# Two gathers and two selections one expert group later, the first later part one group earlier

## The chip, the cores and the metric

The kernel runs on one core of one Trainium2 chip. The metric is the device time of one execution in microseconds, the median of several. The engines are TensorE (PE; its weight loads are PEld), VectorE (DVE), ScalarE (ACT), GpSimd (POOL) and SyncE (SP), which only issues DMAs here. Every engine works through its own list in order, and they meet at semaphores.

## The reference

Two transformer blocks on 256 tokens of width 1024, in float32. The part that matters here is the mixture of experts of the first block. Each token picks one of 4 groups of 8 experts, then the two best experts in it:

```
grp  = argmax(softmax(h @ w_group + b_group))
top_p, top_e = top_k(softmax(in_grp), 2)
weights = p_grp * top_p / sum(top_p)
for each expert e, for its tokens x:
    a = silu(x @ w_gate[e]) * (x @ w_up[e])
    y[token] += weight * (a @ w_down[e])
```

There are 32 experts, w_gate and w_up 1024 x 256 and w_down 256 x 1024 each, so 100 MB of weights for this part. The other stages (projections, mLSTM, attention, the second block with its feed-forward) are not touched.

## The kernel before

The experts are worked through in blocks of 32 tokens. Four blocks side by side fill the 128 columns of a matmul's output, so a group of four experts is one unit. The first 32 tokens of every expert are the groups 0 to 7. An expert with more tokens has further blocks; up to 15 of them stand in the groups 8 to 11, the later groups. `ORDER` (L57) is the order of the twelve: 0, 1, 2, 8, 3, 9, 4, 5, 10, 6, 11, 7; o is the place in it, and two neighbours in it are a pair q.

A normal group is `gate_up(o, k)` for k = 0 to 3 (L1338), each 16 matmuls on one piece of weights, then `hidden_columns` (two transposes of the activation), then `down_rows` (L1414), 32 matmuls on two more pieces. Between these stands `scatter(o - 1)` (L1367), which adds the outputs of the group before to the tokens' rows in PSUM. A later group is cut into three parts: `later_part(g, 0)` and `(g, 1)` are gate and up, `(g, 2)` is `hidden_columns`, a scatter and the down product. `AFTER` (behind the first gate_up of a normal group), `INSIDE` (behind its last) and `BEHIND` (behind its down product) say where they stand (L59 to 61).

The inputs of a pair are gathered by matmuls with a selection matrix: `gather(q, i, b)` (L1296), i = 0 to 3, eight matmuls each, copied out by ACT and DVE in `gathered`. `early_gather` (L1456) waits first until DVE has read the last down product from the two banks that are used again. `GATHERS` (L62) says in which group a pair is gathered. `selects(o)` (L1461) turns the selection matrices of a pair and computes its weights, in the place that `SELECTS` (L63) gives; POOL's `select_pair(q + 2)` (L2284) waits for that and makes the matrices of a later pair.

Weights come in two streams. SP loads 48 pieces of 2 MB, six to a group, in order (L676 to 707). From piece 9 on four slots in `big` take turns (piece 13 alone goes to `dring`), and a piece is issued only when TensorE has used the piece before it in its slot:

```
if n >= SLOTS:
    sp.wait_ge(s_used, slot_before(n) + 1)
```

The weights of a later part are fetched by POOL with indirect DMAs of 128 rows of 8 KB, one for each block, four for a part (three in group 11), in `later_piece(g, k)` (L2303). Where a block is not needed, its index lies out of bounds and its rows bring nothing. The part (8, 0) waits for the seventh piece used, (8, 1) for the fourteenth (numbers 0 to 13: that is the second gate_up of group 2), each further one for the part two before it. POOL's list mixes these issues with `select_pair` (L2318 to 2334). TensorE waits for all blocks of a part in `landed_later` (L1332).

In front of the last two gate_ups of group 7 stand 7 and 13 matmuls on zeros (`filler`), whose only effect is that TensorE is busy.

Of the kernel before, what the change touches and what calls it, by code (L numbers as in the profile page):

```python
# [55 lines left out]
ONCE = SLOTS + RING  # L56
ORDER = [0, 1, 2, 8, 3, 9, 4, 5, 10, 6, 11, 7]  # L57
NLATER = 3
INSIDE = {2: (8, 0), 3: (9, 0), 4: (9, 2), 5: (10, 1), 6: (11, 0), 7: (11, 2)}  # L59
AFTER = {3: (8, 2), 4: (9, 1), 5: (10, 0), 6: (10, 2), 7: (11, 1)}  # L60
BEHIND = {2: (8, 1)}
GATHERS = {1: 1, 2: 2, 3: 3, 4: 4, 6: 5}  # L62
SELECTS = {0: 0, 1: 1, 2: 2, 4: 3, 6: 4, 9: 5}  # L63
LATE = (3, 6, 8, 11)
BESIDE = [(0, 1), (2, 3), (4,), (5,), (6, 7), (8, 9), (10,), (11,)]
NPAIR = NALL // 2
# [86 lines left out]
def build(nc, x, consts, vecs, rows, mod, wa, experts, pieces, wb, ffn, out):  # L153
    with ExitStack() as ctx:
# [162 lines left out]
        def gate_up_done(eng, g):  # L317

            if g < NGRP:
                eng.wait_ge(s_used, NPIECE * g + 4)  # L320
            else:
                eng.wait_ge(s_lused, NLATER * (g - NGRP) + 2)
# [444 lines left out]
        def _(pe):  # L767
# [521 lines left out]
            gathered, downs = {}, []  # L1289
# [166 lines left out]
            def early_gather(q, i):  # L1456

                pe.wait_ge(s_ot, len(downs))
                gather(q, i, 6 + i % 2)
# [10 lines left out]
            for g in range(NGRP):  # L1470
                o = ORDER.index(g)
                q = GATHERS.get(g)
                for k in range(4):
                    if g == NGRP - 1 and k >= 2:
                        pe.wait_ge(s_ot, len(downs))
                        filler(6 * k - 5, 6)
                    gate_up(o, k)
                    if g == 0 and k < 2:
                        gather(0, 2 + k, 6 + k)
                    if k == 0 and g in AFTER:  # L1480
                        later_part(*AFTER[g])
                    if q and k in (1, 2):
                        early_gather(q, k - 1)
                if q and g != 4:
                    early_gather(q, 2)
                    early_gather(q, 3)
                if g in INSIDE:
                    later_part(*INSIDE[g])
                if g == 0:
                    selects(o)  # L1490
                    hidden_columns(o)
                elif g == 4:
                    hidden_columns(o)
                    early_gather(q, 2)
                    early_gather(q, 3)
                    scatter(o - 1)
                    selects(o)
                elif g == NGRP - 1:
                    hidden_columns(o)
                else:  # L1500
                    scatter(o - 1)
                    hidden_columns(o)
                    selects(o)
                down_rows(o)
                if g == NGRP - 1:
                    scatter(o - 1)
                if g in BEHIND:
                    later_part(*BEHIND[g])
# [16 lines left out]
            for i in range(2):  # L1525
                pe.wait_ge(s_cw[i], 16 * (i + 1))
                for j in range(CB // 2):
                    w = ckw[:, j] if i == 0 else cvw[j // 8][:, j % 8]
                    q, at = j % 4, (CB // 2 * i + j) * KVG * NC
# [29 lines left out]
            for t in range(NT):  # L1559
                for h in range(NSAH):  # L1560
                    g, r = h // 3, h % 3
                    q = fmT[g * HD:(g + 1) * HD, 10 + r, t * P:(t + 1) * P]
# [154 lines left out]
        def _(act):  # L1717
# [295 lines left out]
            def gathered(q, i, b):  # L2013

                act.wait_ge(s_ga2, 4 * q + i + 1)
                xg_free(act, q)
                for c in (2 * i, 2 * i + 1):
                    ins = nc.scalar.activation(xg[q % 2][:, c, :], ps[:, b, (c % 2) * T:(c % 2 + 1) * T], ACT.Identity,
                                               scale=modT[:, 40 + c:41 + c], bias=modT[:, 16 + c:17 + c])
                ins.then_inc(s_xa, 1)  # L2020
# [29 lines left out]
            for o, g in enumerate(ORDER):  # L2050
                b = 4 if g < NGRP else 5
                q = GATHERS.get(g)
                if o >= 1 and o not in LATE:
                    outputs_high(o - 1)
                if g == 9:
                    gathered(4, 0, 6)
                if q and g != 4:
                    gathered(q, 0, 6)
                gate_up_done(act, g)
                if o >= 1:  # L2060
                    act.wait_ge(s_hid2, o)
                nc.scalar.activation(hid[:, 0, :], ps[:, b, 0:T], ACT.Tanh, scale=0.5).then_inc(s_hth2, 1)
                if o in LATE and g >= NGRP:
                    outputs_high(o - 1)
                if q and g != 4:
                    gathered(q, 2, 6)
                if o == 0:
                    rows_turned(o)
                act.wait_ge(s_at, o + 1)
                nc.scalar.copy(aT[:, :, :], ps[:, b, 0:T].rearrange("p (f n) -> p f n", f=2)).then_inc(s_atc, 1)  # L2070
                if o in LATE and g < NGRP:
                    outputs_high(o - 1)
                if g == 4:
                    gathered(q, 2, 6)
                if o:
                    rows_turned(o)
            last_high()
# [166 lines left out]
        def _(pool):  # L2244
# [39 lines left out]
            def select_pair(q):  # L2284

                if q >= 1:
                    pool.wait_ge(s_stw, 2 * q)
                for k in range(2):
                    for t in range(NT):
                        for h in range(2):  # L2290
                            g = ORDER[2 * q + h]
                            ins = nc.gpsimd.tensor_scalar(sel12[:, k, t, h * P:(h + 1) * P], const("iota"),  # L2292
                                                          gsp[:, k, t, g:g + 1], None, ALU.is_equal)
                            if (k, t, h) == (1, NT - 1, 1):
                                link(ins)
                            else:
                                link.later(ins)
                if q >= 2:
                    pool.wait_ge(s_ga2, 4 * (q - 1))
                nc.gpsimd.tensor_tensor(sel[:, q % 2, :, :], sel12[:, 0, :, :], sel12[:, 1, :, :], ALU.add  # L2300
                                        ).then_inc(s_sel, 1)

            def later_piece(g, k):  # L2303

                n = later_number(g, k)
                if n == 0:
                    pool.wait_ge(s_used, FIRST.index(6) + 1)
                elif n == 1:
                    pool.wait_ge(s_used, max(SLOTS, ONCE + 1))
                else:  # L2310
                    pool.wait_ge(s_lused, n - 1)
                for b in range(later_blocks(g)):
                    pool.indirect_dma_start(
                        later_slot(n, b), None, later_rows,
                        bass.IndirectOffsetOnAxis(ap=xidx[:, QUAD * (g - NGRP) + b, k:k + 1], axis=0),
                        bounds_check=NE * P * NLATER - 1, oob_is_err=False).then_inc(s_later[n % 2], 16)
# [10 lines left out]
            select_pair(4)  # L2327
            later_piece(9, 2)
            later_piece(10, 0)
            select_pair(5)  # L2330
            later_piece(10, 1)
            later_piece(10, 2)
            for k in range(3):
                later_piece(11, k)
            power(small[:, 24:28], small[:, 24:28], 4, s_ms, 4, s_rstd)
# [10 lines left out]
        def _(dve):  # L2346
# [484 lines left out]
            def gathered(q, i, b):  # L2831

                dve.wait_ge(s_ga2, 4 * q + i + 1)
                xg_free(dve, q)
                for c in (2 * i, 2 * i + 1):
                    ins = V.tensor_scalar(xg[q % 2][:, c, :], ps[:, b, (c % 2) * T:(c % 2 + 1) * T],
                                          modT[:, 40 + c:41 + c], modT[:, 16 + c:17 + c], ALU.mult, ALU.add)
                ins.then_inc(s_xv, 1)
# [48 lines left out]
            for o, g in enumerate(ORDER):  # L2887
                b = 4 if g < NGRP else 5
                q = GATHERS.get(g)
                if o >= 1 and o not in LATE:  # L2890
                    outputs_low(o - 1)
                if g == 9:
                    gathered(4, 1, 7)
                if q and g != 4:
                    gathered(q, 1, 7)
                dve.wait_ge(s_hth2, o + 1)
                if o >= 1:
                    dve.wait_ge(s_at, o)
                link(V.scalar_tensor_tensor(hid[:, 1, :], hid[:, 0, :], 1.0, ps[:, b, 0:T], ALU.add, ALU.mult))
                V.tensor_tensor(hid[:, 1, :], hid[:, 1, :], ps[:, b, T:2 * T], ALU.mult).then_inc(s_hid2, 1)  # L2900
                if o in LATE:
                    outputs_low(o - 1)
                if q:
                    gathered(q, 3, 7)
                if o in SELECTS:
                    p = SELECTS[o]
                    slot_weights(2 * p, 6)
                    slot_weights(2 * p + 1, 7)
# [494 lines left out]
```

## Time and profile before

| | |
|---|---|
| median of 3 runs | 1025.64 us |
| lowest, highest | 1022.02, 1027.52 us |
| the profiled execution | 1023.9 us, span 1022.1 us |
| TensorE busy | 972.6 us, 95% of the span |
| DVE, ACT, POOL busy | 48%, 38%, 37% |
| mean granted clock | 0.98 |
| moved by DMA | 252.08 MB, mean 247 GB/s; by POOL's queue (q0, software) 3.17 MB |

The expert stage lies from about 347 to 570 us of the span. A busy TensorE is no proof that it is the bound: its share is a mean over stages. The page's slices give the engines' busy tenths, the DMA engines' share and the GB/s for 40 equal slices; the timeline of an engine shows in brackets how long it was idle before an instruction and what ended that.

### The profile page before, as it was taken

To read this page: it belongs to the slowest core of one execution; us is meant where nothing else is said; L and a number is where in the kernel's file an instruction comes from. 1 tells how busy PE (TensorE), PEld (TensorE's weight loads), DVE (VectorE), ACT (ScalarE), POOL (GpSimd) and SP (SyncE) were. 2 spreads that over 40 slices of the span, in tenths; PEclk is the share of its full clock that TensorE was granted. 3 is DMA by queue.
4 is the path that set the end of the run, shared out by engine and by line. 5 is a ranking of instruction groups with operands and counts; after the bars stand their busy time and mean duration, and the time that the engine had idled before them with its cause. 6 is when DMAs were issued, how large, how long until landed. Compare 5 with 4: busy or idle time off the path is not lost.

```text
span 1022.1 us, 15203 instructions
## 1 busy us (share of the span) xinstructions
PE 972.6 (95%) x6120; PEld 713.1 (70%) x6120; DVE 492.0 (48%) x853; ACT 385.7 (38%) x617; POOL 379.7 (37%) x249
## 2 busy tenths in 40 slices
PE   7999999999999999898699999999999999999997
PEld 3887777777788544344243699777556789999996
DVE  1445358544244622213031603536665368777775
ACT  1633345445433321111020644544553254434342
POOL 0885747444783055453320499740002500000000
PEclk7999999999999999999799999999999999999999
DMA  9996955334469999999999888533224465454521
GB/s 377 345 414 266 372 172 158 87 100 124 144 208 427 360 425 423 416 398 370 407 407 414 310 321 255 156 93 103 86 80 144 165 268 195 176 204 165 205 82 41
DMA packets 49274, 252.08 MB, mean 247 GB/s; under 512 B 10432, under 2 KB 11072, under 8 KB 31424
## 3 DMA queue, kind: packets, MB, share of 16 engines
q1 hardware_dynamic: 42736, 248.10, 64.4%
q0 software_dynamic: 6480, 3.17, 1.1%
q8 instruction: 41, 0.67, 0.3%
q14 instruction: 17, 0.14, 0.0%
HBM read 294.22 MB, written 1.05 MB: 289 GB/s over the span
## 4 chain that ended last, share of the span: by engine, by line
PE 76%; DVE 7%; issue 6%; DMA 4%; ACT 3%; POOL 2%; DVEq 0%; SPq 0%; POOLq 0%; ACTq 0%
PE ps L885 33%; PE ps L1208 17%; PE ps L1347 3%; PE ps L781 2%; PE ps L1423 2%; PE ps L1362 2%; PE ps L1374 2%; PE ps L833 1%; PE ps L1304 1%; DMA tail<-in_experts_dram,xidx 1%; PE ps L1438 1%; DMA big<-in_pieces_dram 1%; DMA xs<-in_x_dram 1%; PE ps L895 1%; POOL sel L2292 1%
## 5 line engine op out<-in xcount | busy, mean ns | idle before, releaser
L2262 POOL TENSOR_TENSOR wl<-ring,wh 128x1024 fp32r<-128x1024 f32 (+5 forms) x132 | 289.3, 2211 | 228.9 <-ACT wh L1760 227.1
L1760 ACT ACTIVATE wh<-ring 128x1024 fp32r<-128x1024 f32 (+5 forms) x148 | 143.4, 983 | 132.1 <-PE ps L885 100.9
L885 PE MATMUL ps<-wh,hTh 128*128 128x512 f32 (+3 forms) x384 | 153.0, 398 | 1.3 <-DVE wl L3086 1.3
L885 PE MATMUL ps<-wl,hTh 128*128 128x512 f32 (+3 forms) x384 | 148.3, 386 | 0.0
L885 PE MATMUL ps<-wh,hTl 128*128 128x512 f32 (+3 forms) x352 | 136.7, 388 | 0.0
L1208 PE MATMUL ps<-hTs,wsp 128*128 128x256 f32 x1056 | 128.7, 284 | 0.5 <-DVE wsp L2922 0.5
L1208 PEld LDWEIGHTS ps<-hTs,wsp 128*128 128x128 f32 x1056 | 128.1, 192 | 1.5 <-DVE wsp L2922 0.7
L2250 POOL TENSOR_TENSOR small<-small 128x2 f32<-128x2 f32 (+2 forms) x7 | 5.3, 759 | 272.7 <-DVE small L3235 192.4
L885 PEld LDWEIGHTS ps<-wh,hTh 128*128 128x128 f32 x384 | 73.0, 190 | 22.7 <-issue 6.8
L885 PEld LDWEIGHTS ps<-wl,hTh 128*128 128x128 f32 x384 | 73.0, 190 | 13.5
L885 PEld LDWEIGHTS ps<-wh,hTl 128*128 128x128 f32 x352 | 66.8, 190 | 13.4
L1208 PE MATMUL ps<-wsp,aTs 128*128 128x512 f32 x264 | 61.7, 391 | 0.0
L1347 PE MATMUL ps<-big,xg 128*32 128x512 f32 x432 | 53.7, 605 | 7.3 <-DMA big<-in_pieces_dram 7.0
L885 PE MATMUL ps<-hTh,wh 128*128 128x256 f32 x208 | 58.1, 279 | 0.0
L885 PE MATMUL ps<-hTl,wh 128*128 128x256 f32 x208 | 58.0, 279 | 0.0
L885 PE MATMUL ps<-hTh,wl 128*128 128x256 f32 x208 | 57.6, 277 | 0.0
L1976 ACT ACTIVATE wsp<-ring 128x2048 fp32r<-128x2048 f32 x22 | 42.0, 1909 | 40.4 <-PE ps L1208 34.1
L1208 PEld LDWEIGHTS ps<-wsp,aTs 128*128 128x128 f32 x264 | 49.0, 188 | 9.7
L2922 DVE TENSOR_TENSOR wsp<-ring,wsp 128x2048 fp32r<-128x2048 f32 x22 | 50.3, 2285 | 9.5 <-ACT wsp L1976 9.5
L2292 POOL TENSOR_SCALAR sel<-cst,few 128x128 fp32r<-128x128 f32 x40 | 23.3, 596 | 58.6 <-PE ps L1316 58.6
L885 PEld LDWEIGHTS ps<-hTh,wh 128*128 128x128 f32 x208 | 39.1, 188 | 0.8 <-issue 0.8
L885 PEld LDWEIGHTS ps<-hTl,wh 128*128 128x128 f32 x208 | 39.1, 188 | 0.0
(481 smaller groups left out, 1637.3 us busy)
## 6 DMA issues: line engine op xcount, KB each, us to landing
big<-in_pieces_dram SPq DMA_DIRECT2D x42, 2048.0 KB
ring<-in_wa_dram SPq DMA_DIRECT2D x68, 512.0 KB, 3.9
big<-in_mod_dram SPq DMA_DIRECT2D x11, 2048.0 KB, 10.4
ring<-in_ffn_dram SPq DMA_DIRECT2D x11, 2048.0 KB, 9.1
ring<-in_wb_dram SPq DMA_DIRECT2D x40, 512.0 KB, 3.9
dring<-in_ffn_dram SPq DMA_DIRECT2D x11, 1024.0 KB, 4.9
ring<-in_wb_dram SPq DMA_DIRECT2D x12, 384.0 KB, 5.7
dring<-in_pieces_dram SPq DMA_DIRECT2D x2, 2048.0 KB, 21.4
```

The costliest lines, as they stand in the source:

```text
L781: mm = pe.matmul(ps[32 * q:32 * q + 32, 6, :], condw[:, c, :], mtile[n][:, c, :], start=(c < 4), stop=(c >= 4), skip_group_check=True)
L885: mm = pe.matmul(out, x[i], y[j], start=(p, c, k) == (0, 0, 0), stop=(c, k) == (KD - 1, 2), skip_group_check=True)
L1208: mm = pe.matmul(out, w[a], x[b], start=start and n == 0, stop=stop and n == 2, skip_group_check=skip)
L1347: mm = pe.matmul(ps[b * BS:(b + 1) * BS, 4, :], xg[q % 2][:, c, at:at + BS], slot_part(s, b)[:, cc * 512:(cc + 1) * 512], start=(c == 0), ...
L1362: mm = pe.matmul(ps[b * BS:(b + 1) * BS, 5, :], xg[q % 2][:, c, at:at + BS], later_slot(later_number(g, k), b)[:, cc * 512:(cc + 1) * 512] ...
L1374: mm = pe.matmul(ps[:, 2 * t + n, :], selT[:, (o // 2) % 2, o % 2, t * P:(t + 1) * P], x[:, n * 512:(n + 1) * 512], start=False, stop=Fals ...
L1423: mm = pe.matmul(ps[b * BS:(b + 1) * BS, 6 + n, :], aT[:, f, b * BS:(b + 1) * BS], slot_part(s, b)[:, n * 512:(n + 1) * 512], start=(f == ...
L1760: nc.scalar.activation(quarter(name, q, "high"), quarter(name, q, "raw"), ACT.Copy).then_inc(s_qh, 1)
L1976: nc.scalar.activation(wsp[:, 0 if last else m, 0, :], src, ACT.Copy).then_inc(s_hi[m], 1)
L2262: nc.gpsimd.tensor_tensor(quarter(name, q, "low"), quarter(name, q, "raw"), quarter(name, q, "high"), ALU.subtract).then_inc(s_ql, 1)
L2292: ins = nc.gpsimd.tensor_scalar(sel12[:, k, t, h * P:(h + 1) * P], const("iota"), gsp[:, k, t, g:g + 1], None, ALU.is_equal)
L2922: V.tensor_tensor(wsp[:, dst, 1, :], src, wsp[:, dst, 0, :], ALU.subtract).then_inc(s_lo[m], 1)
```

## The change

Two later-part tables change: (8, 0) moves from in front of group 2's down product (INSIDE[2]) to the end of group 1 (BEHIND[1]). The gathers 2 and 3 of the pair 4 move from group 4, behind its hidden columns, to group 5, behind its second and third gate_up; their copies on ACT and DVE move with them. In SELECTS the entry 6: 4 becomes 7: 4, so the two selections of pair 4 (`select_rows` 8 and 9) go from group 4 (o = 6) to group 5 (o = 7). In POOL's list `select_pair(5)` goes behind the issues of (10, 1) and (10, 2).

```diff
-INSIDE = {2: (8, 0), 3: (9, 0), 4: (9, 2), 5: (10, 1), 6: (11, 0), 7: (11, 2)}
+INSIDE = {3: (9, 0), 4: (9, 2), 5: (10, 1), 6: (11, 0), 7: (11, 2)}
 AFTER = {3: (8, 2), 4: (9, 1), 5: (10, 0), 6: (10, 2), 7: (11, 1)}
-BEHIND = {2: (8, 1)}
+BEHIND = {1: (8, 0), 2: (8, 1)}
 GATHERS = {1: 1, 2: 2, 3: 3, 4: 4, 6: 5}
-SELECTS = {0: 0, 1: 1, 2: 2, 4: 3, 6: 4, 9: 5}
+SELECTS = {0: 0, 1: 1, 2: 2, 4: 3, 7: 4, 9: 5}
...
                     if q and k in (1, 2):
                         early_gather(q, k - 1)
+                    if g == 5 and k in (1, 2):
+                        early_gather(4, k + 1)
...
                 elif g == 4:
                     hidden_columns(o)
-                    early_gather(q, 2)
-                    early_gather(q, 3)
                     scatter(o - 1)
                     selects(o)
...
+                if g == 5:
+                    gathered(4, 2, 6)
                 gate_up_done(act, g)
...
-                if g == 4:
-                    gathered(q, 2, 6)
...
             later_piece(10, 0)
-            select_pair(5)
             later_piece(10, 1)
             later_piece(10, 2)
+            select_pair(5)
...
+                if g == 5:
+                    gathered(4, 3, 7)
                 dve.wait_ge(s_hth2, o + 1)
...
-                if q:
+                if q and g != 4:
                     gathered(q, 3, 7)
```

## Rows read from the trace of the kernel before

**Rows 1.** From the page: DMA engines' share in 40 slices, and the pieces' issues.
```profile
DMA  9996955334469999999999888533224465454521
...
big<-in_pieces_dram SPq DMA_DIRECT2D x42, 2048.0 KB
```

**Rows 2.** Windows: length, busy PE, PEld, DVE, ACT, POOL, clock, DMA share, GB/s.
```profile
420.00:430.00 10.00, 9.13 (x68) 3.64 (x72) 2.51 (x2) 1.96 (x3) 2.37 (x3) 0.83 1.02 416
...
445.00:448.00 3.00, 3.00 (x32) 1.10 (x28) 0.84 (x1) 0.00 (x0) 2.92 (x6) 1.00 0.75 246
477.00:480.00 3.00, 3.00 (x34) 1.13 (x30) 0.00 (x0) 0.00 (x0) 3.00 (x6) 1.00 0.43 85
510.00:512.00 2.00, 2.00 (x24) 0.65 (x20) 0.39 (x1) 0.00 (x0) 0.00 (x0) 1.00 0.73 128
```

**Rows 3.** Timeline of SP: start us, length us, queue, line, what it issues.
```profile
427.98 0.37 SPq L701 DMA_DIRECT2D big<-in_pieces_dram  x1
445.43 0.37 SPq L701 DMA_DIRECT2D big<-in_pieces_dram  x1
478.51 0.37 SPq L701 DMA_DIRECT2D big<-in_pieces_dram  x1
510.22 0.37 SPq L701 DMA_DIRECT2D big<-in_pieces_dram  x1
```

**Rows 4.** Timeline of POOL: the first issue of later parts (8,0), (8,1), (8,2), (9,2), (10,1).
```profile
369.81 1.26 POOL L2313 DMA_INDIRECT ring<-in_experts_dram,xidx  x1 [2.87 <-issue]
388.42 1.09 POOL L2313 DMA_INDIRECT dring<-in_experts_dram,xidx  x1 [2.16 <-PE ps L1347]
401.14 0.99 POOL L2313 DMA_INDIRECT ring<-in_experts_dram,xidx  x1 [7.75 <-PE ps L1362]
449.35 1.09 POOL L2313 DMA_INDIRECT dring<-in_experts_dram,xidx  x1 [0.16 <-issue]
482.43 1.09 POOL L2313 DMA_INDIRECT dring<-in_experts_dram,xidx  x1 [0.16 <-issue]
```

**Rows 5.** Timeline of PE in groups 2 and 3.
```profile
383.95 1.93 PE L1347 MATMUL ps<-big,xg 128*32 128x512 f32 x16
392.74 1.92 PE L1347 MATMUL ps<-big,xg 128*32 128x512 f32 x16 [1.01 <-DMA big<-in_pieces_dram]
404.21 3.64 PE L1423 MATMUL ps<-big,aT 128*32 128x512 f32 x32 [0.41 <-ACT selT L2025]
407.64 0.63 PE L1362 MATMUL ps<-dring,xg 128*32 128x512 f32 x2
420.87 5.34 PE L1438 MATMUL ps<-ring,aT 128*32 128x512 f32 x32 [3.45 <-issue]
```

**Rows 6.** The chain that ended last: start us, length us, what it ran through.
```profile
486.41 13.14 DMA tail<-in_experts_dram,xidx
521.79 1.14 PE ps L1304 x8
```

**Rows 7.** Timeline of PE in groups 4, 5 and 7.
```profile
465.90 0.62 PE L1438 MATMUL ps<-dring,aT 128*32 128x512 f32 x2 [0.85 <-issue]
474.76 0.38 PE L1314 MATMUL ps<-cst,selt 128*128 128x128 f32 x2
476.53 3.64 PE L1423 MATMUL ps<-big,aT 128*32 128x512 f32 x32 [0.41 <-ACT selT L2025]
492.38 2.80 PE L1347 MATMUL ps<-big,xg 128*32 128x512 f32 x16 [3.62 <-DMA big<-in_pieces_dram]
499.59 1.07 PE L1362 MATMUL ps<-dring,xg 128*32 128x512 f32 x2 [4.41 <-DMA tail<-in_experts_dram,xidx]
554.12 1.92 PE L1347 MATMUL ps<-big,xg 128*32 128x512 f32 x16
```

**Rows 8.** Timeline of DVE behind the down product of (9, 2).
```profile
469.60 1.28 DVE L2860 SCALAR_TENSOR_TENSOR olt<-ps,few,gateb 128x1024 f32<-128x1024 f32 x1 [4.82 <-PE ps L1438]
472.00 1.23 DVE L2865 TENSOR_TENSOR ol__69<-olt,oh__67 128x1024 fp32r<-128x1024 f32 x1 [1.12 <-ACT oh__67 L2032]
```

## The prediction

> **What bounds the kernel now.** I read the page's slices first, then the ten-microsecond windows, then the queues of SP and POOL, then TensorE in order of time, then the chain. TensorE is busy nearly everywhere, but [rows 1] show the DMA engines full (9 or 8 in every slice from about 310 to 590 us): in the expert stage weights come at some 420 GB/s [rows 2]. A piece is 2048 KB [rows 1], so at 420 GB/s it takes 5.0 us, and 48 pieces take 240 us. The stage ends when the piece stream ends, and the stream is late only by the time in which no piece has been asked for. From 350 us to the last pieces the full windows break three times: 445 to 448 is 0.75 full, 477 to 480 is 0.43, 510 to 512 is 0.73 [rows 2]; that is 0.75, 1.7 and 0.5 us by the share, and with the slow ends of each (a piece asked for at 478.51 finds an engine share that recovers at about 479.8, 1.3 us later) I count 1.3, 2.9 and 1.3 us, 5.5 in all. I number the pieces 0 to 47, six to a group. A piece is asked for when TensorE has finished with the piece before it in its slot; [rows 3] are the issues of pieces 23, 26, 32 and 38. So TensorE sets when pieces are asked for, and the pieces set when it may go on: near the end piece 45 is used at 554.12 [rows 7], right behind 13 fillers, and what comes behind it is TensorE's own.
>
> The later parts are the second resource. POOL issues four blocks for each, and TensorE may use them only when all have landed. The part (8, 1) is first issued at 388.42 [rows 4] and used at 407.64 [rows 5], 19.2 us later, with TensorE's weight load at its wait; (8, 2) is issued at 401.14 and used at 420.87, 19.7 us later and 13.2 us behind the part before, after a stop of 3.45 us; (9, 2) is issued at 449.35 and used at 465.90 [rows 7] after a short stop, 16.5 us; (10, 1) is issued at 482.43 and used at 499.59 after a stop of 4.41 us, 17.1 us. The chain of waits goes through that last one, with 13.14 us from its fourth issue on [rows 6]; POOL could not issue it earlier, as it first made the sixth pair's selection matrices, for which it waits for TensorE's selections.
>
> **The change part by part.** All times are of the profiled execution: span 1022.1, own time 1023.9, which is 1.7 us under the median of 1025.64.
>
> (1) The first later part, (8, 0), comes straight behind the fifth and sixth pieces of group 1, at 383.95, where now group 2 begins [rows 5]. Nothing of its transfer moves: first issue at 369.81 [rows 4]. By the row of (8, 1) it lands at 369.8 + 19.2 = 389.0; by the shortest case, 16.5, at 386.3. So a wait of 2.4 to 5.1 us is added; I take 5.1, since (8, 1) is its neighbour under the same load. Behind it on TensorE stand all of group 2 and every release of a slot. In the trace a stop of 3.45 us is followed by 32 matmuls in 5.34 us against 3.64 for the same count at full clock [rows 5], with a granted clock of 0.83 in 420 to 430 [rows 2], that is, some time at 1.2 GHz; so the part costs 5.3, and TensorE begins group 2 at 394.4, 10.4 us later than now.
>
> (2) What group 2 then loses. Now from 383.95 to its down product at 404.21 are 20.3 us, of which 1.0 is a wait for a piece and 3.6 the part that has left: 15.7 remain, so the down product starts at 410.1, 5.9 late. It ends at 413.5. But (8, 1) is issued only when the second piece of group 2 is used, which is 4.5 us after group 2's start (388.42 less 383.95): at 398.9 instead of 388.4. It lands 19.2 later, at 418.1: a wait of 4.6. With 5.3 for it (slow again) and 1.9 for the next piece, TensorE reaches the scatter in front of (8, 2) at 425.3 and is done with that at 427.6. (8, 2) is issued at some 404 by the order of POOL's queue. It lands at 404 + 19.7 = 423.7 if parts overlap, or 13.2 behind the part before, at 431.3, if they go one after the other. I take 431.3: the longest time from issue belongs to the one part that was issued while its forerunner was under way. Then 5.3 of work: done at 436.6, against 426.2 now: 10.4 late. With the early landing and full clock it is 431.4, 5 late.
>
> (3) What the stream loses. Counting back from 445.5, where it runs dry, by 5.0 a piece and 2.5 for the MB of a real block (POOL's queue moved 3.17 MB in all, the table above has it, so one block of the later groups is real and brings one MB in each of (8, 0), (8, 1) and (8, 2)), piece 17 must follow piece 16 at 395.5 when (8, 1) comes later. It is asked for at 396.4 instead of 385.9 (its slot's piece is the first of group 2, used from 383.95 for 1.93 [rows 5]) and starts 1.3 behind: 2.2 us dry. Piece 22 then ends at 432.7. Piece 23 is asked for when the second piece of group 3 is used, 10.4 later than 427.98, so at 438.4: 7.0 dry. Piece 26, now at 445.43, comes at 455.8, with the stream at 454.7: 2.4 dry. Together 11.6 against 1.3: the stream is 10.3 late at piece 26; by the early ends of (1) and (2) about 2.5 only.
>
> (4) What the other moves give back. In group 4 two gathers (1.14 us each, eight matmuls, [rows 6]) and two selections (with the copy behind them 1.8 us, from 474.76 to 476.53, [rows 7]) leave the stretch in front of the down product that starts at 476.53. What they covered comes out: behind (9, 2)'s down product the output, its high part and its low part (3.7 us from the matmuls' end on DVE and ACT, [rows 8]) must be there for the scatter. (9, 2), issued 10.4 later, lands at 476.3, its product ends at 479.9; 3.7 for the parts and 0.9 for the second half of the scatter give 484.6, so 8.1 late instead of 10.3: the move is worth 2.2. Piece 32 is asked for at 486.6 and the stream is dry for only 0.6 to 0.9 instead of 2.9. In group 5 the two gathers lie where TensorE now waits 3.62 us for piece 33 [rows 7]: free. POOL's sixth pair of selection matrices no longer stands in front of (10, 1), so its transfer is asked for when (9, 2) is done, near 481, and lands near 498; TensorE comes to it at 502 behind piece 33. The stop of 4.41 and its slow matmuls (5.6 for 3.6) go. What is late next is piece 33. The selections then cost their 1.8 in front of the down product of group 5: it starts at 509 to 510 against 507.90, and piece 38 is asked for before the stream, now later, has run dry: 1.3 saved. After that pieces come at 5.0 us each; from the third part of group 6 on TensorE waits for them, as it nearly does now.
>
> **Sum.** Now piece 38 starts 1.3 behind its issue at 510.22, at 511.5, and piece 45 ends eight pieces later, at 551.5. After the change piece 32 starts at 486.6 + 1.3 = 487.9 and 14 pieces follow without a break: piece 45 ends at 557.9, 6.4 later. (By the dry time alone: 2.2 + 7.0 + 2.4 + 0.8 = 12.4 against 5.5, 6.9.) TensorE takes piece 45 2.6 us behind its end now, and waits for piece 33 until 2.6 behind its end (479.8 + 10.0 against 492.38), for the piece at 392.74 until 2.2 behind: 0 to 0.4 of slack, which I take off. +6.0 us. Own time 1029.9; on the median 1031.6.
>
> One place of the Trainium skill speaks for another outcome. The notes, DMA: Bandwidth & Descriptors, section Anatomy of one DMA, give about 2.0 us and bytes / 436e3 for a transfer issued from GpSimd; an estimate by it for four blocks of 1 MB is 11.6 us, and (8, 0) would be there at 381.4, before TensorE asks. This case's trace does not agree: 16.5 to 19.7 us from first issue to use, with a full piece stream beside it. The result of that rule is the first rival, priced below from rows.
>
> **Rivals.** A, faster: (8, 0) has landed at 383.95 (a transfer of 14.1 us or less from its first issue). Then no stop is added, group 2 only exchanges order, (8, 2) is issued earlier, and the late dry spells (2.9 and 1.3) go: 4.2 less, 1021.4. It decides at 383.95. Against it: no row has less than 16.5. For it: no row shows when (8, 0) lands, as it is used long after; and a late start of TensorE may cost less, since 3.45 of waiting in group 3 goes. Chance 0.1. B, even: parts overlap and the stops are short, (8, 2) lands near 424. Then the stream is dry 2.5 to 4 more by piece 26 and gets back 4: -1 to +2.5, 1026.5 in the middle. Chance 0.27. C, the reverse of step (4): the new order does not take the stop at (10, 1) away, because piece 33 and POOL's queue leave it late, and the early loss stands in full: +9 to +10, 1035. Chance 0.13. The forecast itself 0.5.
>
> **Numbers.** A measurement of this kernel tells 0.5% (5.1 us) from no change. The forecast (its own range +3 to +8, 1028.6 to 1033.6) gives 0.32 slower and 0.18 within; B gives 0.26 within and 0.01 faster; C 0.13 slower; A 0.05 faster and 0.05 within. Together faster 0.06, within 0.49, slower 0.45. The range leaves out half of A and the end of C: 1022.5 to 1036.
>
> **What would show it.** Right: TensorE stops some 5 us in front of the first L1362 matmuls, now at about 384, and they take over 5 us; it stops again in front of the next two later parts; SP asks for piece 23 near 438 and the DMA share dips near 433 to 439; the stop at (10, 1) is gone, the dip at 477 is nearly gone; the last filler ends near 560. Wrong: (8, 0) running at 384 without a stop, or a DMA share that stays full from 390 to 445.

## The result, and the profile after

The changed kernel is slower: 1027.56 us in the median of 19 runs against 1022.02 for the kernel before, ratio 1.005 with an interval of 1.0034 to 1.0066, that is 5.1 us (3.5 to 6.7). (One of the 19 executions took 5402.69 us and does not count in the ratio.) The ratio is estimated from the executions of both kernels and need not be the quotient of the two medians; where this text gives a difference in us, it is worked out from the ratio. The profiled execution after has a span of 1023.9 us, only 1.8 more than before. A single pair of executions is a poor measure here: in the one before, TensorE's clock fell to 1.2 GHz twice in the second block, where it did not in the one after. The expert stage itself is 3.8 us longer, counted from the start of group 1's down product to the first matmul on piece 45: 173.60 us before (380.52 to 554.12) and 177.41 after (379.86 to 557.27). The stage began 0.66 us earlier in the execution after, and what follows piece 45 took 1.35 us less there; that is how 3.8 becomes 1.8.

TensorE in order of time, after; the columns are those of [rows 5].

```profile
388.51 6.18 PE L1362 MATMUL ps<-ring,xg 128*32 128x512 f32 x32 [5.01 <-DMA ring<-in_experts_dram,xidx]
394.52 1.89 PE L1347 MATMUL ps<-big,xg 128*32 128x512 f32 x16
...
409.90 3.64 PE L1423 MATMUL ps<-big,aT 128*32 128x512 f32 x32 [0.41 <-ACT selT L2025]
...
416.57 0.62 PE L1362 MATMUL ps<-dring,xg 128*32 128x512 f32 x2 [3.03 <-DMA tail<-in_experts_dram,xidx]
...
429.81 3.64 PE L1438 MATMUL ps<-ring,aT 128*32 128x512 f32 x32 [1.75 <-issue]
...
473.34 0.62 PE L1438 MATMUL ps<-dring,aT 128*32 128x512 f32 x2 [2.58 <-issue]
...
479.55 1.17 PE L1374 MATMUL ps<-oh__67,selT 128*128 128x512 f32 x4 [2.21 <-ACT oh__67 L2032]
...
481.85 3.64 PE L1423 MATMUL ps<-big,aT 128*32 128x512 f32 x32
...
496.74 1.92 PE L1347 MATMUL ps<-big,xg 128*32 128x512 f32 x16 [0.25 <-DMA big<-in_pieces_dram]
498.48 0.60 PE L1362 MATMUL ps<-dring,xg 128*32 128x512 f32 x2
...
505.98 3.86 PE L1423 MATMUL ps<-big,aT 128*32 128x512 f32 x32 [0.41 <-ACT selT L2025]
...
512.77 3.33 PE L1347 MATMUL ps<-big,xg 128*32 128x512 f32 x16 [2.94 <-DMA big<-in_pieces_dram]
...
557.27 1.92 PE L1347 MATMUL ps<-big,xg 128*32 128x512 f32 x16
```

TensorE stops 5.01 us in front of (8, 0) and the part's 32 matmuls then take 6.18 us. Group 2 starts at 394.52 instead of 383.95. (8, 1) and (8, 2) are waited for as well (3.03, 1.75), (9, 2) for 2.58. Where the row says "<-issue", the view names no cause; that the wait in front of (8, 2) is for its transfer can be read from the landing: its last block landed at 429.61, and the matmuls start at 429.81. In the same way (8, 0) landed at 388.47 and (8, 1) at 416.52. The scatter of group 4 waits 2.21 us for the output that the two gathers and the selections had covered. The stop of 4.41 at (10, 1) [rows 7] is gone, and of the wait of 3.62 for piece 33 only 0.25 is left. In their place TensorE now waits 2.94 us at 512.77 for piece 36, the first of group 6, and the 16 matmuls behind that wait take 3.33 us instead of 1.9. Group 6 had no such wait before.

The clock at the first stop, then the DMA engines in the windows where they now have too little to do; columns as in [rows 2].

```profile
386.00:394.00 8.00, 5.49 (x28) 1.33 (x32) 1.19 (x1) 0.00 (x0) 0.00 (x0) 0.57 1.01 425
...
394.00:400.00 6.00, 6.00 (x56) 2.26 (x52) 0.00 (x0) 0.69 (x2) 1.03 (x1) 1.00 0.68 233
432.00:438.00 6.00, 6.00 (x56) 2.32 (x48) 2.51 (x2) 2.08 (x3) 3.13 (x3) 1.00 0.54 155
450.00:456.00 6.00, 5.59 (x55) 2.27 (x58) 1.92 (x5) 0.72 (x3) 5.52 (x9) 1.00 0.72 240
484.00:487.00 3.00, 3.00 (x32) 0.91 (x28) 1.28 (x1) 0.13 (x1) 0.00 (x0) 1.00 0.99 252
...
380.00:556.00 176.00, 152.57 (x1167) 65.71 (x1164) 40.61 (x70) 26.69 (x50) 64.96 (x77) 0.96 0.98 397
```

The same before, with the whole of each dip of [rows 2]:

```profile
442.00:450.00 8.00, 7.59 (x75) 3.46 (x77) 2.36 (x6) 2.06 (x4) 6.60 (x10) 1.00 0.90 353
476.00:482.00 6.00, 5.59 (x54) 2.12 (x57) 1.85 (x5) 0.82 (x2) 5.69 (x9) 1.00 0.64 206
509.00:514.00 5.00, 4.62 (x42) 1.24 (x34) 1.32 (x2) 1.07 (x2) 0.57 (x1) 1.00 0.86 274
...
380.00:556.00 176.00, 154.69 (x1191) 67.78 (x1190) 40.97 (x72) 27.04 (x51) 65.09 (x77) 0.96 0.99 406
```

Two dips are new (near 396 and 434), the one at 452 is the old one of 445, that of 477 [rows 2] has shrunk to a short one at 485, and that of 510 has gone. The granted clock of 0.57 around the stop says that most of that stretch was at 1.2 GHz; TensorE had been idle for 5 us in it. By the bytes that are missing against 420 GB/s the four dips are 2.7, 3.8, 2.6 and 1.2 us, 10.2 together, against 1.3, 3.1 and 1.7 before, 6.1: 4.1 us of dry stream more. Over the whole of 380 to 556 us the mean fell from 406 to 397 GB/s, which is 3.8 us of a full stream, as much as the stage is longer.

The issues of SP and POOL that follow from it (after): piece 23, asked for at 427.98 before [rows 3], piece 26 (445.43) with the two behind it, piece 32 (478.51); then the first issues of (8, 0), (8, 1), (8, 2) and (10, 1) [rows 4].

```profile
435.22 3.38 SPq L701 DMA_DIRECT2D big<-in_pieces_dram  x2
...
452.67 3.80 SPq L701 DMA_DIRECT2D big<-in_pieces_dram  x3
...
483.83 0.37 SPq L701 DMA_DIRECT2D big<-in_pieces_dram  x1
```

```profile
369.16 1.26 POOL L2313 DMA_INDIRECT ring<-in_experts_dram,xidx  x1 [2.87 <-issue]
...
398.97 1.09 POOL L2313 DMA_INDIRECT dring<-in_experts_dram,xidx  x1 [13.38 <-PE ps L1347]
...
404.25 0.99 POOL L2313 DMA_INDIRECT ring<-in_experts_dram,xidx  x1 [0.30 <-issue]
...
477.79 0.98 POOL L2313 DMA_INDIRECT dring<-in_experts_dram,xidx  x1 [11.05 <-PE ps L1438]
```

POOL waited 13.38 us for the second piece of group 2 before it could ask for (8, 1); before, 2.16 us [rows 4]. Piece 23 was asked for 7.2 us later, and that is the dip at 434. And (10, 1) was asked for at 477.79 instead of 482.43, with nothing of POOL's matrices in front of it.

The two stretches of the second block in which the clock fell before (same columns):

```profile
680.00:686.00 6.00, 6.00 (x26) 4.29 (x25) 3.14 (x8) 2.47 (x10) 0.14 (x1) 0.72 0.00 0
...
769.00:774.00 5.00, 4.44 (x12) 3.45 (x13) 4.69 (x9) 0.00 (x0) 0.00 (x0) 0.66 0.64 269
```

In the execution after, the clock is 1.00 in both windows. That part of the kernel is the same program in both, so the profiled execution of before was a little unlucky there.

### The profile page after: what moved, and what is told of

Read it like the earlier page. It is cut to its first block, busy times and chain, and to the rows that moved or that the text cites. A ratio compares the mean times of both kernels' runs of the same rounds, so it can differ in the third digit from the quotient of the medians.

```text
span 1023.9 us, 15195 instructions
## 1 busy us (share of the span) xinstructions
PE 968.2 (95%) x6112; PEld 709.4 (69%) x6120; DVE 493.8 (48%) x853; ACT 385.6 (38%) x617; POOL 380.2 (37%) x249
## 4 chain that ended last, share of the span: by engine, by line
PE 74%; DMA 10%; DVE 8%; issue 4%; ACT 3%; POOL 1%; DVEq 0%; SPq 0%; POOLq 0%; ACTq 0%
PE ps L885 31%; PE ps L1208 17%; DMA big<-in_pieces_dram 4%; PE ps L1347 4%; PE ps L1362 2%; PE ps L781 2%; DMA ring<-in_wa_dram 2%; PE ps L1374 2%; PE ps L1423 2%; DMA ring<-in_experts_dram,xidx 1%; PE ps L833 1%; PE ps L1438 1%; DMA tail<-in_experts_dram,xidx 1%; PE ps L1304 1%; DMA xs<-in_x_dram 1%
## 5 line engine op out<-in xcount | busy, mean ns | idle before, releaser
L885 PEld LDWEIGHTS ps<-hTh,wl 128*128 128x128 f32 x208 | 39.6, 191 | 0.0
```

Of the source, the lines that this page charges most:

```text
L885: mm = pe.matmul(out, x[i], y[j], start=(p, c, k) == (0, 0, 0), stop=(c, k) == (KD - 1, 2), skip_group_check=True)
```

## The experiments

The theory: (8, 0) in front of group 2 makes TensorE wait for a transfer, and what stands behind it (the releases of group 2's slots, hence (8, 1), (8, 2), the pieces) comes late; the late moves bring something. The main rival: the late moves are what costs. The runs stand in three series, each on a chip of its own with the kernel before beside it: rest_only, part_only, mid_part and one_block in the first, fill_stop, select_only, gather_only and mid_only in the second, rest_again, mid_again and select_mid in the third. All ratios are to the kernel before of the same series, with their 95% intervals. "Stage" is the time from the start of group 1's down product to the first matmul on piece 45 in the one profiled execution, 173.60 us before. One execution can lie several us beside the median: use the stage to see where time goes, and the ratio for how much.

**Late moves alone (rest_only, rest_again).** Against the changed kernel:

```diff
-INSIDE = {3: (9, 0), ...
-BEHIND = {1: (8, 0), 2: (8, 1)}
+INSIDE = {2: (8, 0), 3: (9, 0), ...
+BEHIND = {2: (8, 1)}
```

> The change without its first part: (8, 0) stays in front of group 2's down product; the two gathers, the two selections and POOL's order are moved. Theory (the loss is the stop in front of (8, 0)): faster than the kernel before by 2 to 4 us (0.2 to 0.4%), no stop at (10, 1), the dip of the DMA share at 477 to 480 shorter by 2 us. Rival 1 (the late moves cost: the scatter of group 4 has lost its cover): slower than before by 1 to 5 us. Rival 2 (the late moves do nothing, as the stream covers them): within 1 us of before.

Measured: 1020.21 against 1023.53, ratio 0.9974 (0.9963 to 0.9984), 2.7 us faster; stage 168.22 us. TensorE, in the place where the stops at piece 33 and (10, 1) were, has one short wait, and after it the down product of group 5 starts at 496.35 instead of 507.90:

```profile
487.11 1.92 PE L1347 MATMUL ps<-big,xg 128*32 128x512 f32 x16 [1.17 <-DMA big<-in_pieces_dram]
...
496.35 3.64 PE L1423 MATMUL ps<-big,aT 128*32 128x512 f32 x32 [0.41 <-ACT selT L2025]
```

Rival 1 falls: the late moves do not cost. The profiled execution was the fastest of its 13 (1015.47 us), so a stage of 168.22 is too good. The second run, in the third series:

> The late moves alone, a second time, beside the next two on one chip: -2 to -4 us against before.

Measured: 1018.52 against 1023.62, 0.9946 (0.9927 to 0.9966), 5.5 us faster, more than expected; the two intervals only just meet (0.9963 to 0.9966). So the worth of the late moves is some 3 to 5 us, and two series can differ by about as much as an interval is wide; stage 171.75 this time, in the slowest of the 10 executions. The expected shorter dip at 477 to 480 is seen in the first of the two traces (none is left there) and not in the second:

```profile
476.00:482.00 6.00, 6.00 (x51) 1.92 (x53) 1.28 (x1) 0.10 (x1) 0.66 (x1) 0.95 0.60 168
```

What both have is that the stop at (10, 1) and the dip at 510 are gone; both wait for piece 36 instead (2.21 and 2.95 us).

**(8, 0) alone (part_only).** The kernel before with only

```diff
-INSIDE = {2: (8, 0), 3: (9, 0), ...
-BEHIND = {2: (8, 1)}
+INSIDE = {3: (9, 0), ...
+BEHIND = {1: (8, 0), 2: (8, 1)}
```

> The kernel before with only the move of (8, 0) to the end of group 1. Theory: slower than the kernel before by 6 to 9 us (0.6 to 0.9%), more than the whole change, with a stop of 5 us at 384, dips of the DMA share near 396, 434 and 453, and the stop at (10, 1) kept or turned into one behind pieces. Rival 1 (the late moves are what costs): within 1 us of before. Rival 2 (late moves do nothing): the same as the whole change, +5 us.

Measured: 1030.14 against 1023.53, 1.0062 (1.0045 to 1.0079), 6.3 us slower, more than the whole change; stage 180.50. The stop and the slow matmuls, and two of the dips:

```profile
389.28 6.43 PE L1362 MATMUL ps<-ring,xg 128*32 128x512 f32 x32 [4.83 <-DMA ring<-in_experts_dram,xidx]
```

```profile
396.00:399.00 3.00, 3.00 (x32) 0.69 (x24) 0.00 (x0) 0.00 (x0) 0.00 (x0) 1.00 0.26 63
484.00:487.00 3.00, 3.00 (x32) 1.09 (x28) 0.00 (x0) 0.00 (x0) 3.00 (x6) 1.00 0.41 82
```

The dip at 484 is that of 477 [rows 2] moved on by 7 us: without the late moves nothing of it is given back. The stop at (10, 1) is kept, as expected, and is 5.30 us long. The two halves do not quite add up: +6.3 with -2.7 or -5.5 gives +3.6 or +0.8, less than the +5.1 of the whole; with the intervals the first fits and the second hardly.

**(8, 0) two gate_ups later (mid_part, mid_again).** The changed kernel with

```diff
-BEHIND = {1: (8, 0), 2: (8, 1)}
+BEHIND = {2: (8, 1)}
...
+                    if (g, k) == (2, 1):
+                        later_part(8, 0)
```

> The whole change, but (8, 0) stands behind the second gate_up of group 2, so that the piece that (8, 1) waits for is used first. Theory: TensorE comes to (8, 0) at 387.5, waits about 1.5 us, full clock after it, (8, 1) is issued at 388.4 as before: the loss is gone, 1 to 4 us faster than the kernel before. Rival 1: as slow as the whole change, +5 us. Rival 2: as the kernel before.

Measured: 1019.52 against 1023.53, 0.995 (0.993 to 0.9971), 5.1 us faster, a little more than expected; stage 170.72.

```profile
389.25 3.64 PE L1362 MATMUL ps<-ring,xg 128*32 128x512 f32 x32 [1.60 <-DMA ring<-in_experts_dram,xidx]
```

A stop of 1.60 and full clock after it. The wait for the transfer ends near 389, as in the changed kernel; 3.6 us of work put in front of the wait, and with it the piece that (8, 1) waits for, turn +5 into -5. The second run:

> The late moves with (8, 0) behind the second gate_up of group 2, a second time. If the place of (8, 0) is worth something by itself beside the late moves, 1 to 3 us faster than the late moves alone; if the 2.4 us between the two in the first call were noise, the same as they.

Measured: 1018.3 against 1023.62, 0.9935 (0.9911 to 0.996), 6.6 us faster; the late moves alone gave 0.9946 in the same series. The intervals overlap widely: the place of (8, 0) has no worth that this shows.

**One block instead of four (one_block).** The changed kernel, with three empty transfers of (8, 0) left out:

```diff
                 blocks = sum(later_blocks(NGRP + m // NLATER) for m in range(n % 2, n + 1, 2))
+                if n % 2 == 0:
+                    blocks -= QUAD - 1
...
-                for b in range(later_blocks(g)):
+                for b in range(1 if n == 0 else later_blocks(g)):
```

> The whole change, but POOL issues only the first of the four blocks of (8, 0) and TensorE waits for that one; the other three bring nothing in either kernel. Theory: the block lands near 380.5, no stop at 384, group 2 begins at 387.4 with full clock, (8, 1) is issued at 392 instead of 399; the result is at or below the kernel before, -3 to 0 us. Rival 1: +5 us as the whole change, without the stop. Rival of mechanism (the stop is harmless, what costs is that group 2's releases come 3.6 us later because of the part's own matmuls): +3 to +5 us.

Measured: 1022.08 against 1023.53, 0.9993 (0.9978 to 1.0007), 0.7 us faster; stage 174.73.

```profile
384.38 3.64 PE L1364 MATMUL ps<-ring,xg 128*32 128x512 f32 x32
387.81 1.93 PE L1349 MATMUL ps<-big,xg 128*32 128x512 f32 x16
...
424.77 6.13 PE L1440 MATMUL ps<-ring,aT 128*32 128x512 f32 x32 [3.83 <-issue]
```

```profile
392.29 1.09 POOL L2315 DMA_INDIRECT dring<-in_experts_dram,xidx  x1 [5.60 <-PE ps L1349]
```

```profile
431.00:434.00 3.00, 3.00 (x28) 1.44 (x24) 1.87 (x2) 1.26 (x2) 1.98 (x2) 1.00 0.44 74
```

The stop is gone, and some 5.8 us of the loss with it (+5.1 has become -0.7, the two in different series), so the wait was for this transfer, and for its empty blocks: the last packet of the one real block ended at 380.70. But the kernel still has only 0.7 of the 3 to 5 us that the late moves bring. (8, 1) is asked for at 392.29 instead of 388.42, as (8, 0)'s own 3.6 us lie in front of group 2, (8, 2) still stops TensorE for 3.83, and the stream is dry at 431 to 434. So the rival of mechanism holds a part: the order costs some 2 to 4 us even without the stop. (In the same series rest_only is 1.9 us faster than this kernel, with intervals that just overlap, and mid_part 4.4 us, with intervals apart.)

**Busy during the stop (fill_stop).** The changed kernel with

```diff
+                if g == 1:
+                    pe.wait_ge(s_ot, len(downs))
+                    filler(16, 6)
                 if g in BEHIND:
                     later_part(*BEHIND[g])
```

> The whole change, with a wait for DVE's read of the down product and 16 matmuls on zeros in front of (8, 0), so that TensorE is busy during most of the stop. Theory, with the clock as a part of the loss: the stop itself stays (group 2 cannot begin before (8, 0) has landed near 388.5), but the 32 matmuls of (8, 0) take 3.6 us instead of 6.2 and the granted clock stays at 2.4 GHz there: 1 to 2.5 us faster than the whole change, so +2.5 to +4 against the kernel before. Rival (only the wait matters, the clock does not reach the end): +5 us as the whole change.

Measured: 1026.06 against 1023.13, 1.0028 (1.0013 to 1.0043), 2.9 us slower; stage 174.79.

```profile
384.27 3.40 PE L895 MATMUL ps<-zero 128*128 128x512 bf16 x15 [1.63 <-DVE olt L2863]
387.95 3.64 PE L1362 MATMUL ps<-ring,xg 128*32 128x512 f32 x32 [0.28 <-DMA ring<-in_experts_dram,xidx]
```

```profile
384.00:392.00 8.00, 7.45 (x55) 2.81 (x60) 1.23 (x1) 1.06 (x1) 0.74 (x1) 1.00 1.01 424
```

The clock stays at 1.00, the part takes 3.64 instead of 6.18. That 2.5 us are saved at the place is shown. The end says about 2.2 us (1.005 against 1.0028), as was expected, but the two ratios come from different series and their intervals overlap: that some 2 us of the loss are the clock that falls behind the stop is likely, not shown.

**The late moves one by one (select_only, gather_only).** The kernel before with only `SELECTS` and POOL's `select_pair(5)` moved:

> The kernel before with only the selections of pair 4 and POOL's sixth pair of matrices one group later; the gathers stay in group 4, (8, 0) stays in group 2. Theory: the stop at (10, 1) goes, and 1.8 us leave the stretch in front of group 4's down product, of which most is taken by the wait for the output; piece 32 is asked for 1 to 1.5 us earlier: 1.5 to 2.5 us faster than before. Rival: all of the gain of the late moves is in the gathers, 0 to -0.5 us here.

Measured: 1020.21 against 1023.13, 0.9967 (0.9947 to 0.9986), 3.4 us faster, more than expected; stage 170.88. (10, 1) is asked for at 470.44, and TensorE uses it at 490.99 without a wait:

```profile
470.44 0.99 POOL L2313 DMA_INDIRECT dring<-in_experts_dram,xidx  x1 [12.50 <-PE ps L1438]
```

```profile
490.99 0.60 PE L1362 MATMUL ps<-dring,xg 128*32 128x512 f32 x2
```

The gain does not come by the whole of the expected way. Group 4's down product starts 95.9 us into the stage against 96.0 before, and piece 32 is asked for at 97.9 against 98.0: in these two executions the selections that have left group 4 bring nothing there. What is won is won behind, at (10, 1). With only the gathers moved:

> The kernel before with only the two gathers moved to group 5. Theory: the gathers leave group 4 (2 us and 1 us of wait), but the stop at (10, 1) stays, with POOL's selection matrices earlier by the same 1 to 2 us: 0.5 to 2 us faster than before. Rival: the stop at (10, 1) eats it, within 0.5 us.

Measured: 1022.41 against 1023.13, 0.9994 (0.9976 to 1.0012), no difference; stage 173.53. The wait for piece 33 is gone, and the stop at (10, 1) has grown from 4.41 to 6.02 us, as the expectation's rival had it:

```profile
498.31 1.07 PE L1362 MATMUL ps<-dring,xg 128*32 128x512 f32 x2 [6.02 <-DMA tail<-in_experts_dram,xidx]
```

So the gain of the late moves is that of the selections and POOL's order, moved together; which of the two it is was not tried apart. The gathers alone only move TensorE ahead to a wait that they cannot shorten.

**The middle place alone (mid_only), and with the selections (select_mid).** The edits are those above, on the kernel before.

> The kernel before with only (8, 0) moved behind the second gate_up of group 2. Theory: if the place is harmless and frees the ring slots for (8, 2) no earlier in effect, 0 to -1 us against before, since the gain of 5 us seen with all moves together comes from the late ones (2.7 measured) and from an earlier (8, 2) (up to 2). Rival: the place itself brings 2 us or more by itself.

Measured: 1024.13 against 1023.13, 1.0007 (0.9992 to 1.0023), no difference, as expected. The trace shows why an earlier (8, 2) is worth nothing. It is asked for 7 us earlier than before (401.14) and used no earlier than before (420.87):

```profile
394.19 0.99 POOL L2315 DMA_INDIRECT ring<-in_experts_dram,xidx  x1 [0.30 <-issue]
```

```profile
421.33 5.34 PE L1438 MATMUL ps<-ring,aT 128*32 128x512 f32 x32 [3.14 <-issue]
```

> Only the selections late, and (8, 0) behind the second gate_up of group 2; the gathers stay in group 4. If the gain is all in the selections and POOL's order, the same as the other two, -3 to -4 us against before; if the gathers add a part, 1 us behind the run above.

Measured: 1017.74 against 1023.62, 0.9948 (0.9924 to 0.9972), 5.3 us faster, like the other two of its series, and more than expected. The three are one result: some 0.5% faster than the kernel before and 1% faster than the changed one, and the only part they share is the selections with POOL's order. The simplest version that beats both kernels is therefore select_only.

## Why the prediction was right

The forecast was +6.0 us by a stop in front of (8, 0), with what the late moves give back already taken off; the runs gave +5.1 (3.5 to 6.7), and part_only, mid_part and one_block show the cause to be the place of (8, 0) and the stop in front of it. On the median the forecast was 1031.6 and 1027.56 was measured; 3.6 of those 4.0 us are the kernel before, whose median was 1025.64 in 3 runs and 1022.02 in 19. Between slower and no clear change the forecast was undecided (0.45 and 0.49, with the line at 0.5%), and the measured +0.5% lies on that line. Step by step:

(1) The stop was taken as 5.1 us, and it is 5.01; the landing of the transfer was read off its neighbour's row (19.2 us from first issue, here 369.16 to 388.51, 19.3). The slow matmuls were taken as 5.3 and are 6.18. The low price of 2.4 us for the stop, and rival A with it, are out. So is the landing at 381.4 that the prediction estimated by the Trainium skill (DMA: Bandwidth & Descriptors, section Anatomy of one DMA): beside a full piece stream the four blocks need 19 us, three of them empty; with the one real block alone (one_block) TensorE finds it there at 384.38.

(2) Group 2 was forecast to start at 394.4 and its down product at 410.1; they start at 394.52 and 409.90. (8, 1) was issued at 398.97 (forecast 398.9) but landed at 416.5, not at 418.1: 17.6 us from its issue instead of 19.2. (8, 2) came at 429.8, 13.2 us behind (8, 1), so that the parts go one after the other is borne out, against 423.7 if they overlapped. (8, 1)'s matmuls were slow as forecast: 5.15 us, to 421.72. Those of (8, 2) took 3.64, not 5.3: the clock did not fall behind the stop of 1.75. These two sizes are where the forecast was off: 436.6 forecast for the end of (8, 2), 433.24 measured.

(3) The stream, by missing bytes: the dip at piece 17 was forecast as 2.2 us and is 2.7, that at piece 23 as 7.0 and is 3.8, that at piece 26 as 2.4 and is 2.6, the one at piece 32 as 0.8 and is 1.2. The term that was mis-sized is the one at 23, by 3.2 us, and that is (2) again: piece 23 was asked for at 435.22 instead of 438.4. Piece 26 came at 452.67 (forecast 455.8). Together 10.2 against the forecast 12.4, with 6.1 against 5.5 for the kernel before: 4.1 more instead of 6.9.

(4) The scatter's lost cover was forecast and is there (2.21 us). Group 4's down product was forecast at 484.6 and starts at 481.85, piece 32 at 486.6 and comes at 483.83, the down product of group 5 at 509 to 510 and starts at 505.98: the same 3 us early throughout. The stop at (10, 1) went, as said, and rival C fell. Its transfer was not there near 498 as forecast but at 487.56, since it met the dip at 485. The wait of 2.94 us for piece 36 is in no step. In the stage of the profiled pair the sum is +3.8 instead of +6.0. That the medians differ by 5.1 and so lie nearer to 6.0 is not explained by that pair: the mechanism was right, and the closeness of the number is in part luck.

Rival B (an even result) had the right idea of the size being smaller but the wrong mechanism, overlap, which the 13.2 us deny. The late moves were counted in step (4) as some 3.4 us of dry stream (2.9 down to 0.8, and 1.3); by themselves they measure 2.7 and 5.5. What the prediction did not see is that the gathers by themselves bring nothing (gather_only), and that the selections, by select_only's trace, bring their gain at (10, 1) and none in group 4.

Left open: the sum of the halves. +6.3 and -2.7 to -5.5 give +0.8 to +3.6, and the whole measures +5.1. Whether the late moves are worth less behind the early stop (their gain is in dips that a later stream has partly filled) or the difference is the spread between series was not tried.

## What to carry to other kernels

A consumer that is moved ahead in an in-order engine must be held against the landing of its data, read off a row of the same kind of transfer under the same load; the 3.6 us of work that stood in front of the wait here decided between +5 and -5 us. Count then what is queued behind the stop: besides TensorE's own time these are the slot releases, each of which started another transfer late, and the stream lost as many bytes as fit the longer stage (3.8 us). And before gathers, copies or other covers are moved, ask which list holds up the transfer that is waited for: here a piece of work stood in front of it on the engine that issues it, and moving that, with the selections that it waits for, brought the gain, while moving the gathers brought nothing.

## What the runs showed of the hardware

Transfers of indirect rows that are out of bounds bring no data and still take their time. POOL's queue has fewer packets with three of (8, 0)'s four blocks left out (one_block, second row) than in the changed kernel, and moves the same bytes:

```profile
q0 software_dynamic: 6480, 3.17, 1.1%
q0 software_dynamic: 6048, 3.17, 1.0%
```

In the trace's records of these packets 384 carry 8 KB, which is the real block of (8, 0), (8, 1) and (8, 2); an empty row is a packet of 4 bytes that takes 9 ns. Yet the packets of an empty block are spread over some 2.5 to 3 us while the piece stream is full ((9, 2) after: 464.03 to 466.54, then to 469.34), and over 0.1 to 0.2 us where the stream is dry ((10, 1) after: 484.44 to 484.58, then to 484.76). A real block beside the full stream took 5.2 us ((8, 1) before: 392.64 to 397.88). So an empty block costs about half of a real one: with three blocks left out the part was there at 384.38 or before, with them at 388.47, and TensorE waited for the empty ones. From first issue to use a part with one real block took 17.6 to 19.7 us and one of four empty ones 16.5 to 17.1, beside the full stream.

Two parts do not overlap. (8, 2) was used 13.2 us behind (8, 1) both before and after, though its first issue lay 12.7 us behind the other's before and 5.3 after. Its first packet moves when the last of (8, 1) does: 405.83 and 406.07 before, 415.05 and 415.35 after.

How long TensorE may stand still before its clock falls cannot be told from the length of the stop. Behind a stop of 1.60 us (mid_part) the clock stayed, behind one of 5.01 us (after) it fell; but in gather_only it fell behind 1.78 us (16 matmuls in 3.53 us for 1.92) and stayed behind 3.11 us:

```profile
391.73 3.53 PE L1347 MATMUL ps<-big,xg 128*32 128x512 f32 x16 [1.78 <-DMA big<-in_pieces_dram]
...
421.18 3.64 PE L1438 MATMUL ps<-ring,aT 128*32 128x512 f32 x32 [3.11 <-issue]
```
